# FOX's values projected ahead of attention, positions on the partitions, and five weight units per cycle

## The reference

```python
for l in range(DEPTH):
    h = rms_norm(x, norm_g[l])
    proj = jnp.einsum('btd,dc->btc', h, w_in[l])
    q_a, kv_a, g_a, z_a, q_b, k_b, v_b, f_b, z_b, merge = jnp.split(proj, split_at, axis=-1)
    y_a = nsa_mixer(q_a, kv_a, g_a, ...) * jax.nn.silu(z_a)
    y_b = fox_mixer(q_b, k_b, v_b, f_b, b_forget[l]) * jax.nn.silu(z_b)
    r_a, r_b = jnp.split(merge, 2, axis=-1)
    merged = (jax.nn.sigmoid(r_a) * jnp.einsum('btc,cd->btd', y_a, w_proj_nsa[l])
              + jax.nn.sigmoid(r_b) * jnp.einsum('btc,cd->btd', y_b, w_proj_fox[l]))
    x = x + jnp.einsum('btd,de->bte', merged, w_out[l])
return rms_norm(x, final_g)
```

## Time and profile before

| | |
|---|---|
| time, median of 3 runs (lowest to highest) | 1452.71 us (1452.62 to 1452.74) |
| the profiled execution: its own time | 1452.71 us |
| its span, first to last instruction | 1451.0 us |
| PE busy | 1441.9 us, 7550 matmuls |
| DVE busy | 1045.8 us |
| ACT busy | 911.8 us |
| POOL busy | 465.5 us |
| granted TensorE clock, mean | 0.999 |

### The profile page before, as it was taken

The page is one execution under the profiler, slowest core; times in us unless marked ns, Lnnn a source line. Parts: engine busy times, 40 slices in busy tenths (PEclk is TensorE's granted clock), DMA queues, the critical chain, the costliest instruction groups (busy, mean ns, idle before and its releaser), DMA issues.

```text
span 1451.0 us, 24707 instructions
## 1 busy us (share of the span) xinstructions
PE 1441.9 (99%) x7550; PEld 1231.4 (85%) x7550; DVE 1045.8 (72%) x2422; ACT 911.8 (63%) x1904; POOL 465.5 (32%) x578
## 2 busy tenths in 40 slices
PE   9999999999999999999999999999999999999998
PEld 7888888888888888888888888888888888888887
DVE  6888888888888874444578888888888887643444
ACT  6677777777877752223365877877877876522234
POOL 2435545445445310000023445445445444000000
PEclk9999999999999999999999999999999999999999
DMA  9222222221222243333453222222222212433332
GB/s 285 68 67 59 59 58 59 59 55 51 56 58 59 56 134 95 93 101 90 109 187 79 62 53 59 58 59 59 59 59 58 57 45 59 145 96 102 92 102 91
DMA packets 213890, 117.97 MB, mean 81 GB/s; under 512 B 9304, under 2 KB 212272, under 8 KB 213296
## 3 DMA queue, kind: packets, MB, share of 16 engines
q1 hardware_dynamic: 211408, 107.49, 27.3%
q0 software_dynamic: 1728, 8.66, 1.6%
q10 hardware_dynamic: 672, 0.83, 0.2%
HBM read 110.54 MB, written 6.42 MB: 81 GB/s over the span
## 4 chain that ended last, share of the span: by engine, by line
PE 97%; ACT 1%; DVE 1%; issue 0%; POOL 0%; DVEq 0%; POOLq 0%; ACTq 0%
PE acc L1824 68%; PE turned L1899 7%; PE o_pair L1924 7%; PE scores L1884 4%; PE scores L1886 4%; PE turned L2074 1%; PE misc L1943 1%; PE o_pair L1932 1%; PE scores L1824 1%; PE misc L1847 1%; PE o_pair L1958 0%; PE acc L2189 0%; PE o_pair L2189 0%; ACT w_hi L815 0%; PE o_pair L2091 0%
## 5 line engine op out<-in xcount | busy, mean ns | idle before, releaser
L1824 PE MATMUL acc<-u_hi,w_hi 128*128 128x512 f32 x1096 | 432.5, 395 | 0.0
L1824 PE MATMUL acc<-u_lo,w_hi 128*128 128x512 f32 x1096 | 430.4, 393 | 0.0
L1824 PE MATMUL acc<-u_hi,w_lo 128*128 128x512 f32 x1096 | 428.0, 393 | 0.0
L944 ACT ACTIVATE prob<-prob,row_max 128x384 f32<-128x384 f32 (+3 forms) x384 | 215.2, 560 | 140.1 <-DVE row_max L1409 135.8
L1226 DVE TENSOR_TENSOR w_lo<-w_raw,w_hi 128x1024 fp32r<-128x1024 f32 x184 | 229.7, 1249 | 80.7 <-ACT w_hi L815 79.2
L738 POOL TENSOR_SCALAR prob<-prob,row_inv,gates 128x256 f32<-128x256 f32 (+3 forms) x256 | 170.3, 666 | 264.1 <-DVE row_inv L1416 263.4
L815 ACT ACTIVATE w_hi<-w_raw 128x1024 fp32r<-128x1024 f32 x184 | 193.8, 1054 | 94.3 <-PE acc L1824 88.0
L1824 PEld LDWEIGHTS acc<-u_lo,w_hi 128*128 128x128 f32 x1096 | 206.0, 188 | 39.0 <-issue 0.2
L1824 PEld LDWEIGHTS acc<-u_hi,w_lo 128*128 128x128 f32 x1096 | 205.8, 188 | 37.9
L1824 PEld LDWEIGHTS acc<-u_hi,w_hi 128*128 128x128 f32 x1096 | 206.0, 188 | 37.0 <-issue 0.2
L1409 DVE CUSTOM_DVE_ANT_0 prob<-scores,causal 128x384 f32<-128x384 f32 (+3 forms) x384 | 185.1, 482 | 38.3 <-PE scores L1886 23.0
(11 more groups left out here) (276 smaller groups left out, 2340.1 us busy)
## 6 DMA issues: line engine op xcount, KB each, us to landing
w_raw<-in_w_in_dram SPq DMA_DIRECT2D x140, 512.0 KB, 3.8
w_raw<-in_w_proj_nsa_dram SPq DMA_DIRECT2D x16, 512.0 KB, 3.7
w_raw<-in_w_proj_fox_dram SPq DMA_DIRECT2D x16, 512.0 KB, 3.7
w_raw<-in_w_out_dram SPq DMA_DIRECT2D x16, 512.0 KB, 3.6
x_scratch<-xT POOLq DMA_DIRECT2D x2, 2048.0 KB, 8.7
xT<-x_scratch POOLq DMA_DIRECT2D x2, 2048.0 KB, 8.6
x_nat<-in_x_dram SPq DMA_DIRECT2D x4, 512.0 KB, 6.8
c_w<-in_cmp_w_k_dram SPq DMA_DIRECT2D x4, 512.0 KB, 5.8
```

Of the source, the lines that this page charges most:

```text
L944: act.activation(prob[:, ring, 0:width], prob[:, ring, 0:width], ACT.Exp, bias=row_max[:, ring:ring + 1], scale=-1.0, accum_out=row_sum[:, ...
L1824: ins = pe.matmul((bank or acc[par])[0:width, :], own_w, rhs, start=(n == 0), stop=(n == 23))
```

## The change

FOX's values are projected before the cycles, as `x` transposed times `v_b`'s columns, so that positions come out on the partitions and nothing has to be turned. One half at a time: 4 pairs (512 columns), four banks for the four position tiles, 4 units of two k-tiles each (`values`, units 9 to 16 of the layer); ACT and DVE read the banks with the row's `rstd_t` into `v_all` (and `v_last` for the last pair), which take the place of `v_fox`. In layer 1 `rstd_t` is made with four small transposes. `z_a`'s first unit becomes number 17. The second half's banks are `acc[0]`, `misc`, `o_pair` and `turned[0]`. The writes of `vcb` and of the second `v_pair` move ahead of the cycles too.

A cycle then has five units (the last three, and two of the merge), and `Plan` levels 120 unit matmuls over the 24 slots, not 144. For the last cycle it adds 2.5 to the cost of every slot from 9 on. Unit matmuls in slots 0 to 23 of a middle cycle are now 8 3 8 0 8 4 7 5 8 0 7 0 8 6 7 5 8 0 6 1 9 4 7 1, units beginning in slots 0, 4, 8, 14, 18. In the last cycle (28 slots) they were 7 4 7 0 8 4 7 5 8 0 6 0 8 6 7 5 8 0 6 1 8 4 7 2 9 5 9 3 and are 8 4 8 1 8 5 7 6 8 0 5 0 6 4 5 3 6 0 4 0 6 2 5 0 7 4 7 1. All cycles are unrolled on all engines.

```diff
-U_CYCLE, U_MERGE, U_OUT, U_ALL = 10, 56, 88, 96
+U_VALUES, U_CYCLE, U_MERGE, U_OUT, U_ALL = 9, 18, 56, 88, 96
+V_CHUNKS = 4
+CYCLE_UNITS = 5
+KEY_SLOT = 9
...
-        self.cum = spread(24 * 6, busy)
+        if last:
+            busy = [b if s < KEY_SLOT else b + 2.5 for s, b in enumerate(busy)]
+        self.cum = spread(24 * CYCLE_UNITS, busy)
         self.begin, self.end = {}, []
-        for u in range(6):
+        for u in range(CYCLE_UNITS):
...
+            v_all = sb("v_all", [P, 2, PAIRS, T], F32R)
-            v_fox = sb("v_fox", [P, 2, QT, 2 * HD], F32R)
+            v_last = sb("v_last", [P, 2, T], F32R)
...
+        def cycles(l, body):
+
+            for i in range(PAIRS):
+                body(Cycle(l, i, i // (PAIRS // GROUPS), first=i == 0, last=i == PAIRS - 1,
+                           next_g=min(i + 1, PAIRS - 1) // (PAIRS // GROUPS)))
+        def values_banks(half):
+
+            return (turned[0], turned[1], scores[1], scores[0]) if half == 0 else (acc[0], misc, o_pair, turned[0])
...
@@ block.sync
+            def load_values(l, n, half, par):
+
+                ks, col = slice(2 * (n % V_CHUNKS), 2 * (n % V_CHUNKS) + 2), C_VB + T * (n // V_CHUNKS)
+                sp.wait_ge(w_lo_done, 2 * half + par + 1)
+                apart(sp)
+                sp.dma_start(w_raw[:, par, :, :].rearrange("p (k j) c -> p k (j c)", k=2).unsqueeze(1),
+                             w_view[:, bass.ds(l, 1), ks, bass.ds(col, T)]).then_inc(w_landed[par], 16)
...
@@ block.scalar, body
-                v, z = (2, 3) if cycle.last else (3, 4)
-                at(plan.end[v] + 3, lambda: v_round(l * 10 + 2 + i, v_fox[:, :, :, 0:HD]))
+                z = 2 if cycle.last else 3
...
@@ block.scalar, ahead of the cycles
+                def values_high(half, t):
+
+                    if t < QT - 1:
+                        act.wait_ge(vf_mm, (QT - 1) * (2 * l + half) + t + 1)
+                    else:
+                        act.wait_ge(unit_mm, l * U_ALL + U_VALUES + V_CHUNKS * (half + 1))
+                    for src, to in values_parts(half, t):
+                        ins = act.activation(to[..., 0:HD], src, ACT.Copy, scale=rstd_t[:, t:t + 1])
+                    ins.then_inc(vf_hi_done, 1)
...
+                split_hi(*kv(13))
+                act.wait_ge(f_saved, 32 * (l + 1))
+                if l:
+                    act.wait_ge(rstd_column, l)
+                values_high(0, 0)
+                split_hi(*kv(14))
+                for t in range(1, QT):
+                    values_high(0, t)
+                for n in (15, 16, 17):
+                    split_hi(*kv(n))
+                for t in range(QT - 1):
+                    values_high(1, t)
+                split_hi(*kv(18))
+                values_high(1, QT - 1)
...
@@ block.vector, body
-                v, z = (2, 3) if cycle.last else (3, 4)
-                at(plan.end[v] + 1, lambda: v_of(*cycle.unit(v), v_raw[:, :], [(v_turned, l * 10 + 2 + i)]))
+                z = 2 if cycle.last else 3
...
-                at(plan.end[v] + 4, lambda: v_rest(l * 10 + 2 + i, v_fox[:, :, :, HD:2 * HD], v_fox[:, :, :, 0:HD]))
...
@@ block.vector, ahead of the cycles
-                v_rest(l * 10, v_pair[:, :, 0, :, HD:2 * HD], v_pair[:, :, 0, :, 0:HD])
                 k_rest(q_rope, [(0, 1), (1, 1)], l * 26 + 2)
                 split_lo(*kv(10))
-                z_raw_of(*kv(9), 2 * PAIRS * l, 0)
+                v_rest(2 * l, v_pair[:, :, 0, :, HD:2 * HD], v_pair[:, :, 0, :, 0:HD])
...
+                def values_low(half, t):
+
+                    dve.wait_ge(vf_hi_done, 2 * QT * l + QT * half + t + 1)
+                    whole, *rest = values_parts(half, t)
+                    by_head = [(whole[0][:, h], whole[1][:, h]) for h in range(2)]
+                    for src, to in by_head + rest:
+                        ins = dve.scalar_tensor_tensor(to[..., HD:2 * HD], src, rstd_t[:, t:t + 1], to[..., 0:HD],
+                                                       ALU.mult, ALU.subtract)
+                    ins.then_inc(vf_lo_done, 1)
...
@@ block.tensor, body
-                def turn():
-                    pe.wait_ge(v_lo_done, l * 10 + 2 + i)
-                    turn_v(l * 10 + 2 + i, v_raw)
-
-                extra.setdefault(plan.end[2 if cycle.last else 3] + 2, []).append(turn)
...
@@ block.tensor, ahead of the cycles
+                if l:
+                    for qt in range(QT):
+                        pe.transpose(misc[:, 2 * P + 32 * qt:2 * P + 32 * qt + 32], rstd[0:32, P * qt:P * qt + P],
+                                     ident[0:32, 0:32])
...
+                    for t in range(QT):
+                        bank, cols = values_banks(part)[t], slice(P * t, P * t + P)
...
+                        for j in range(2):
+                            for m, (u, w) in enumerate(((u_hi, 0), (u_lo, 0), (u_hi, 1))):
+                                ins = pe.matmul(bank[:, :], u[:, 2 * c + j, cols], w_of[w][:, j, :],
+                                                start=(c, j, m) == (0, 0, 0), stop=(c, j, m) == (V_CHUNKS - 1, 1, 2))
...
+                values(0)
+                values(1)
+                pe.wait_ge(v_lo_done, 2 * l + 1)
+                turn_v(2 * l + 1, z_silu[:, 1, :])
+                for n in range(2, 2 * V_CHUNKS):
+                    values(n)
+                unit_piece(0, 24, *divmod(l * U_ALL + U_CYCLE - 1, 2), free=(v_raw_done, 2 * l + 1))
```

More of the change, by code:

```diff
@@ L470, in key_cols, with fox_values, values_parts @@
             return P * (qt + 1)
[L472 to L484, removed]
+        def cycles(l, body):
+            for i in range(PAIRS):
+                body(Cycle(l, i, i // (PAIRS // GROUPS), first=i == 0, last=i == PAIRS - 1,
+                           next_g=min(i + 1, PAIRS - 1) // (PAIRS // GROUPS)))
+        def fox_values(i, stream, kt):
+            cols = slice(2 * HD * kt, 2 * HD * kt + 2 * HD)
+            return v_last[:, stream, cols] if i == PAIRS - 1 else v_all[:, stream, i + 1, cols]
+        def values_banks(half):
+            return (turned[0], turned[1], scores[1], scores[0]) if half == 0 else (acc[0], misc, o_pair, turned[0])
+        def values_parts(half, t):
+            first = 2 * HD * t
+            bank = values_banks(half)[t][:, :].rearrange("p (i h c) -> p h i c", i=V_CHUNKS, h=2)
+            if half == 0:
+                return [(bank, v_all[:, :, 1:1 + V_CHUNKS, first:first + 2 * HD])]
+            return [(bank[:, :, 0:V_CHUNKS - 1], v_all[:, :, 1 + V_CHUNKS:PAIRS, first:first + 2 * HD]),
+                    (bank[:, :, V_CHUNKS - 1], v_last[:, :, first:first + 2 * HD])]
         def keys(pair, stream):
@@ new lines, in _ @@
+                vcb_upper((0, 1, 2, 3))
+                split_lo(*kv(11))
+                vcb_lower((0, 1, 2, 3))
+                v_rest(2 * l + 1, v_pair[:, :, 1, :, HD:2 * HD], v_pair[:, :, 1, :, 0:HD])
+                split_lo(*kv(12))
+                split_lo(*kv(13))
+                dve.wait_ge(f_saved, 32 * (l + 1))
+                values_low(0, 0)
+                split_lo(*kv(14))
+                for t in range(1, QT):
+                    values_low(0, t)
+                for n in (15, 16, 17):
+                    split_lo(*kv(n))
@@ L1653, in _ @@
+                for t in range(QT - 1):
+                    values_low(1, t)
+                split_lo(*kv(18))
+                values_low(1, QT - 1)
+                z_raw_of(*kv(17), 2 * PAIRS * l, 0)
+                cycles(l, body)
                 merge0 = half0 + U_MERGE // 2
@@ L1872, in score_step @@
                             pe.wait_ge(f_landed, 32 * (pair.m + 1))
+                    if s == 0 and cycle.first and pair is nsa:
+                        pe.wait_ge(vf_lo_done, 2 * QT * l + QT)
                     if 0 in parts and not (cycle.first and pair is nsa and s < 2):
@@ L1895, in turn_step @@
                     pe.wait_ge(s_scaled, pair.s0 + s + 1)
+                    if cycle.first and pair is nsa and s == 0:
+                        pe.wait_ge(vf_lo_done, 2 * QT * (l + 1))
                     if not (cycle.first and pair is nsa and s < 2):
@@ L1939, in cmp_scores @@
                     pe.wait_ge(cb_ready, CB_PARTS * l + 2)
[L1940 removed]
+                    if cycle.first:
+                        pe.wait_ge(vf_lo_done, 2 * QT * (l + 1))
                     apart(pe)
```

132 lines of the change are left out of this document (74 added, 58 removed).

## The result

| | before | after |
|---|---|---|
| time, median (lowest to highest) | 1452.66 us (1452.46 to 1452.74) | 1470.03 us (1469.61 to 1470.42) |
| ratio, 95% interval | | 1.012 (1.0102 to 1.0137) |
| span of the profiled execution | 1451.0 us | 1468.2 us |
| a middle cycle, start to start | 56.07 us | 51.55 us |

A forecast was written before the change was run, and what follows sets the result against it. PE (TensorE), busy 1441.9 of 1451.0 us, was taken to bound the kernel, plus whatever it waits. 1452.7 - 7.0 + 0.4 + 0.3 + 15.4 - 2.0 = 1459.8 us, 0.5% slower; range 1447 to 1471.

The forecast's parts named there:

- Turns removed, -7.0: Cycles: 16 turns of v_raw go, each saving 0.44 us of PE by the spacing of starts, -7.0 us.
- The rival that they cost their records (-17.4): v_raw's 64 transposes cost their 272 ns records, so 17.4 us go instead of 7.0: 1449.4 us; chance 0.02.
- Loops, 0: Middle cycles: removing the Fori loops saves nothing, since cycles inside and outside a loop last 56.07 to 56.08 us.
- Value stage, +0.7 for both layers: Ahead of the cycles: +0.4 us for layer 1's small rstd transposes, +0.3 for PE waiting on w_lo at unit 10.
- Middle cycles, +15.4: PE waits 1.28 us for pt_lo at the turn of step 6 in each of 12 middle cycles, +15.4 us.
- First cycles, 0: First cycle of each layer: no wait, since it splits its q_fox rounding and its vcb operations go; 0.
- Last cycles, -2.0: Last cycle of each layer: the old wait of 1.0 us goes, as the first ten slots hold more units; -2.0 us.
- 0 in the sum, up to +1 each: Last cycles' later slots: DVE's 23.6 busy us fit in 28.9, so no wait summed, up to +1 us each in the range.
- The second wait (1471): Middle cycles' end: PE also waits at turn 23 for POOL's scaling or behind slot 18, 11 us more: 1471; chance 0.15.
- The chain keeps up (1444.4): Middle cycles: ACT and DVE's chain takes 9.1 us instead of 10.4, PE waits nowhere: 1444.4 us; chance 0.17.

The follow-up runs named there:

- turns_twice: Kernel before, with the four transposes of v_raw done twice over in each of 16 cycles: 1459.46 us, 6.9 more.
- early_unit0: Changed kernel with 4 unit matmuls of first and middle cycles brought forward into slots 0 to 3, so unit 0 ends sooner: 1461.23 us, 8.8 less.
- before_placed: Kernel before, its six units and turns kept, with unit matmuls of first and middle cycles placed as in the changed kernel up to slot 8: 1470.96 us, ratio 1.0128.
- late_split: Changed kernel with the split of unit 2's weights moved from slot 4 to slot 5 in every cycle: 1463.16 us, 6.9 less.
- two_roundings: Changed kernel with the rounding of q_fox in two slots in all cycles, not only the first and last: 1461.61 us, 8.4 less.
- last_even: Changed kernel with 12 unit matmuls of the last cycle moved from slots 24 to 27 into slots 10 to 21: 1469.91 us, 0.1 less.
- light_last: Changed kernel whose last cycles leave out rounding 448 of 512 columns of FOX's keys, less work for DVE and ACT, none off PE: 1466.98 us, 3.05 less.
- six_last: Changed kernel with two_early's edits and z_a projected in its own cycle, giving the last cycle six units: 1448.94 us, ratio 0.9975 to the kernel before.
- two_early: Changed kernel with the edits of two_roundings and early_unit0 together: 1454.70 us, ratio 1.0015 to the kernel before.

## Why the prediction was right or wrong

- **Turns removed, -7.0.** Held: turns_twice gives 6.9 for the same 64 transposes. The rival that they cost their records (-17.4) is out, and with it the time worked out from the Trainium skill's 275 ns (TensorE: Matmul & The Clock Gate, Part 4: PE-mode transpose): in this kernel's full stream of PE the records are 272 ns long, and a turn removed saves 0.11 us.
- **Loops, 0.** Held.
- **Value stage, +0.7 for both layers.** Not seen: the stretches ahead of the cycles grew by 42.80 + 43.45 us for 380 matmuls, which at 0.228 us are 86.6, so 0.4 us less than no cost at all. Of that, 0.3 lies at the kernel's start, where this execution was quicker by as much; the other executions of the changed layout have the start of before. No wait appeared at unit 10.
- **Middle cycles, +15.4.** The mechanism, its place, its releaser and nearly its size held: 1.34 us at turn 6 of all twelve, 1.4 with what lies around it, so 16.7. early_unit0 and before_placed show that the place of the unit matmuls makes it, late_split and two_roundings that the chain is the one named.
- **First cycles, 0.** Wrong by 0.9 each. The wait at turn 6 is absent there, but short ones stand at turns 8 and 16 (in the changed kernel's timeline 0.26 and 0.41 us). I had looked for one wait and not for the next in line.
- **Last cycles, -2.0 and "0 in the sum, up to +1 each" for the later slots.** This is the step that failed. The old waits at turns 8 and 9 shrank, but to 0.4 us and not to nothing; the later slots lost 3.5 us each. Together that is 3.9 us in each last cycle and 7.7 in all, where the sum had 0. I had compared sums: DVE 23.6 busy us in 28.9. That is the argument which the prediction itself set aside for the middle cycles in its first part ("averages don't show its tightest place"). In slots 10 to 16 the line through DVE and ACT sets the pace, and part of the matmuls that had covered it was gone: slots 11 to 27 hold 28 fewer, since the change shifts matmuls to slots ahead of 9 besides taking a unit out. Busy time does not show it even afterwards: from 495.72 to 527.44 DVE is busy for 22.47 of 31.72 us and ACT for 21.68. last_even, light_last and six_last show it from three sides. What sets the waits at the very end of a last cycle (y_all at 519.23, L762 at 522.97), which light_last left as they were, no run takes apart.
- **The second wait (1471).** The time came out there, but not by that way: the changed kernel has no wait at turn 23 or behind slot 18 of a middle cycle, and with the first wait removed none appeared (cycles of 50.2 us in two_early). The rival was wrong although its number was close.
- **The chain keeps up (1444.4).** Wrong as the change stands; it is what a middle cycle does once the chain is shortened at two places.

In short: the forecast was right where it followed a chain instruction by instruction, and wrong, for the most part, in the one place where it added up busy time.

## What to carry to other kernels

When work leaves the engine that bounds a kernel, look for the waits which that work had covered, and walk each stage's chain instruction by instruction, also in the stages that run only once in a layer (here the last cycle, which held three quarters of the miss); count the matmuls between the two ends of each chain rather than busy shares. Before such a change is given up, move the placement: here edits of a few lines turned +1.2% into +0.15%, and a unit put where PE had to wait anyway made it -0.25%. The engine named as releaser (POOL here, busy 40% of the time in that window) may only be the end of a line whose slow members are others.

## What was not expected of the hardware

Nothing new in kind. Transposes of 128x128 in a full stream cost 0.107 us each by doubling them, a fifth more than the 0.088 between their starts in one group of four.

The spacing of 128x512 matmuls is not one number. In the stretch of the earlier trace rows the nine steps from 64.32 to 66.40 are 0.231 us each and the twelve from there to 69.12 are 0.227, which gives the 0.2286 of the prediction. The value matmuls, with positions as the stationary side, do the same after four transposes: ten steps of 0.231 us (63.76 to 66.07), then 0.227 (66.30 to 74.23). So the side that is stationary makes no difference here; the first matmuls after another kind are spaced a little wider. Why, no run shows.
